# Merge, queries and everything behind as one stage, the queries' norm taken tile by tile

## The reference

```
n = rmsnorm(h); [ssd | gdn | gates] = n @ w_in
h += ( sigmoid(g_a) * (ssd_mixer(...) @ w_ssd_out)
     + sigmoid(g_b) * (gdn_mixer(...) @ w_gdn_out) ) @ w_out          # the merge
t = rmsnorm(h, norm_ffn)
qry = t @ w_query                                                     # 2048 wide
s = einsum(qry, sub_keys); top 16 of each half, top 16 of the 256 sums, softmax gate
h += sum over the chosen experts of  gelu(t . expert_u) * gate * expert_v
h += sigmoid(rmsnorm(h, norm_ple) @ w_ple_gate) * (p @ w_ple_proj);   y = rmsnorm(h)
```

## Time and profile before

| what | value |
|---|---|
| median of 3 runs | 2361.13 us (2359.95 to 2368.63) |
| the profiled execution | 2365.91 us |
| its span | 2364.0 us |
| TensorE busy | 2264.0 us (96%) |
| VectorE busy | 1542.0 us (65%) |
| GpSimd busy | 1205.3 us (51%) |
| ScalarE busy | 872.1 us (37%) |
| mean granted TensorE clock | 0.985 of full |

### The profile page before, as it was taken

One profiled execution on the slowest core, in us unless ns is written; L12 is line 12 of the kernel. 1 busy time (PEld: TensorE's weight loads), 2 busy tenths in 40 slices (PEclk: granted clock), 3 DMA queues, 4 the chain that ended last, 5 costly groups with the idle time before them and its releaser, 6 DMA issues.

```text
span 2364.0 us, 31147 instructions
## 1 busy us (share of the span) xinstructions
PE 2264.0 (96%) x10852; PEld 1883.7 (80%) x10852; DVE 1542.0 (65%) x3515; ACT 872.1 (37%) x1305; POOL 1205.3 (51%) x979
## 2 busy tenths in 40 slices
PE   8999899899989998899999999999999999999998
PEld 6787777788878886688888888888878888888885
DVE  4553688677764442119888888884238888887783
ACT  6454433244434331334333333333233323323342
POOL 3333465666544432324566666665647765555510
PEclk9999999999999999999999999999999999999999
DMA  4222011223345231324444444446449999999940
GB/s 166 89 82 79 19 45 40 82 86 128 133 150 180 89 125 36 127 78 126 143 146 147 147 147 141 145 144 215 147 143 384 392 382 347 364 347 356 355 188 36
DMA packets 160314, 394.61 MB, mean 167 GB/s; under 512 B 27376, under 2 KB 93168, under 8 KB 149872
## 3 DMA queue, kind: packets, MB, share of 16 engines
q1 hardware_dynamic: 125424, 326.32, 40.1%
q0 software_dynamic: 34816, 67.41, 7.6%
HBM read 328.45 MB, written 65.21 MB: 167 GB/s over the span
## 4 chain that ended last, share of the span: by engine, by line
PE 58%; DMA 0%; ACT 0%; issue 0%; DVE 0%; POOL 0%; DVEq 0%; SPq 0%
PE ps L182 10%; PE ps L181 10%; PE ps L180 10%; PE ps L2246 7%; PE ps L2247 7%; PE ps L2248 7%; PE ps L1316 4%; PE ps L1578 1%; PE ps L2298 1%; DMA query_slots_sb<-peer_query 0%; POOL query_low_sb L1284 0%; PE ps L2276 0%; DVE h_sb L2121 0%; ACT query_high_sb L1272 0%; DVE ple_gate_sb L2110 0%
## 5 line engine op out<-in xcount | busy, mean ns | idle before, releaser
L1801 POOL DMA_INDIRECT g_dense<-up_gates_summed_sb,up_gate_at_sb x384 | 418.9, 1091 | 300.7 <-issue 222.5
L180 PE MATMUL ps<-n_high_sb,up_u_high_sb 128*128 128x512 f32 x1024 | 398.4, 389 | 0.0
L182 PE MATMUL ps<-n_high_sb,up_u_low_sb 128*128 128x512 f32 x1024 | 398.4, 389 | 0.0
L181 PE MATMUL ps<-n_low_sb,up_u_high_sb 128*128 128x512 f32 x1024 | 398.3, 389 | 0.0
L2246 PE MATMUL ps<-down_v_high_sb,down_w_high_sb 128*128 128x512 f32 x768 | 300.2, 391 | 4.8 <-issue 4.8
L2247 PE MATMUL ps<-down_v_low_sb,down_w_high_sb 128*128 128x512 f32 x768 | 299.8, 390 | 0.0
L2248 PE MATMUL ps<-down_v_high_sb,down_w_low_sb 128*128 128x512 f32 x768 | 299.7, 390 | 0.0
L1660 DVE TENSOR_TENSOR up_u_low_sb<-up_u_sb,up_u_high_sb 128x1024 fp32r<-128x1024 f32 x128 | 156.6, 1224 | 159.0 <-ACT up_u_high_sb L1822 158.7
L2174 ACT ACTIVATE down_v_high_sb<-down_v_sb 128x1024 fp32r<-128x1024 f32 x120 | 125.8, 1048 | 310.4 <-PE ps L2248 310.4
L1834 ACT ACTIVATE up_gelu_sb<-ps 128x512 f32<-128x512 f32 x128 | 76.5, 598 | 406.5 <-PE ps L182 406.4
L181 PEld LDWEIGHTS ps<-n_low_sb,up_u_high_sb 128*128 128x128 f32 x1024 | 192.2, 188 | 39.9
(11 more groups left out here) (348 smaller groups left out, 4747.9 us busy)
## 6 DMA issues: line engine op xcount, KB each, us to landing
up_u_sb<-expert_u SPq DMA_DIRECT2D x128, 512.0 KB, 3.8
down_v_sb<-expert_v SPq DMA_DIRECT2D x32, 2048.0 KB, 11.9
a_dense<-up_gelu_sb SPq DMA_DIRECT2D x128, 256.0 KB, 2.2
g_dense<-nought_sb SPq DMA_DIRECT2D x8, 3072.0 KB, 10.7
down_gelu_sb<-a_dense SPq DMA_DIRECT2D x32, 768.0 KB, 4.8
down_gates_sb<-g_dense SPq DMA_DIRECT2D x32, 768.0 KB, 6.3
w_slots_sb<-w_conv SPq DMA_DIRECT2D x19, 1024.0 KB, 4.9
query_slots_sb<-peer_query SPq DMA_DIRECT2D x8, 1024.0 KB, 5.0
```

The lines of the kernel that those rows point to most:

```text
L180: pe.matmul(out, ah, bh, start=k == 0, stop=False)
L181: pe.matmul(out, ah, bl, start=False, stop=False)
L182: last = pe.matmul(out, al, bh, start=False, stop=k == n - 1)
L1801: pool.indirect_dma_start(cells, at, summed[:, tt, k:k + 1], None).then_inc(stored[tt], 16)
```

## The change

`merge_stage` becomes `merge_programs`: the same programs for the five engines, but handed to `down_stage`, where each engine runs its merge program ahead of its up program in the same block. The barrier between them goes. Waits take its place: query weights are loaded and their high parts made once the mixing products are done (`mixed_in`), the low parts once `m_low` is complete, and the keys once all merge products are done. The output product waits for merged tiles one by one. The norm of the queries is a new class, `FfnNorm`: the last four adds of the merge are made inside its program, each followed by that tile's square, mean, root, reciprocal and two half scalings. Its scaled tiles have memory of their own, so that the query weights don't overlap them. In the up part, the gelus of the first two down blocks are loaded at block 108, and the gates where both were loaded before.

```diff
-            def free_out(tt, p):
-                if tt == 0:
-                    pe.wait_ge(m_low, KT)
-            for p in (OUT, OUT + 1):
-                stream.pe(pe, p, 4 * (p - OUT), lambda tt: free_out(tt, p), (mh, ml), True)
+        merged = lambda kt: pe.wait_ge(m_low, kt + 1)
+        stream.pe(pe, OUT, 0, lambda tt: None, (mh, ml), True, merged)
+        stream.pe(pe, OUT + 1, 4, lambda tt: None, (mh, ml), True)
...
+class FfnNorm(NormT):
+    def act(self, act, merge):
+        m = self.m
+        for tt in range(TT):
+            act.wait_ge(merge.added, TT + tt + 1)
+            act.activation(self.xs[:, tt, :], m.h[:, tt, :], ACT.Square,
+                           accum_out=m.stat[:, 0, tt:tt + 1]).then_inc(self.sq_done, 1)
+            act.wait_ge(self.ms_done, tt + 1)
+            act.activation(m.stat[:, 2, tt:tt + 1], m.stat[:, 1, tt:tt + 1], ACT.Sqrt).then_inc(self.root_done, 1)
...
+    def dve(self, dve, merge):
...
+        def scale(tt):
+            dve.wait_ge(self.root_done, tt + 1)
+            st.done(dve.reciprocal(m.stat[:, 0, tt:tt + 1], m.stat[:, 2, tt:tt + 1]))
+            for half in range(2):
+                c = slice(half * CW, (half + 1) * CW)
+                dve.tensor_scalar(self.xs[:, tt, c], m.h[:, tt, c], m.stat[:, 0, tt:tt + 1], None, ALU.mult).then_inc(self.scaled, 1)
+
+        merge.add(dve, 1, 0)
+        mean(0)
+        scale(0)
+        merge.add(dve, 1, 1)
+        mean(1)
+        for tt in range(2, TT):
+            merge.add(dve, 1, tt)
+            scale(tt - 1)
+            mean(tt)
+        scale(TT - 1)
...
+    def pe(self, pe, merge):
...
+        for half in range(2):
+            for tt in range(TT - 1):
+                if half:
+                    pe.wait_ge(merge.added, 2 * TT)
+                else:
+                    pe.wait_ge(merge.added, TT)
+                pe.wait_ge(self.scaled, 2 * tt + 2)
+                for kt in range(half * KT // 2, (half + 1) * KT // 2):
+                    turn(tt, kt)
+        for kt in range(KT):
+            pe.wait_ge(self.scaled, 2 * (TT - 1) + 1 + kt // (KT // 2))
+            turn(TT - 1, kt).then_inc(self.turned, 1)
...
     def sp(self, sp):
-        sp.dma_start(self.keys[:, :, :], ...).then_inc(self.keys_in, 16)
-        self.stream.sp(sp)
+        def keys(n):
+            if n == 2:
+                sp.wait_ge(self.merge.prod, self.merge.all_products)
+                sp.dma_start(self.keys[:, :, :], ...).then_inc(self.keys_in, 16)
+
+        sp.wait_ge(self.merge.prod, self.merge.mixed_in)
+        self.stream.sp(sp, keys)
...
     def act(self, act, split):
-        self.norm.act(act, between=lambda: (self.stream.high(act, 0), self.stream.high(act, 1)))
+        act.wait_ge(self.merge.prod, self.merge.mixed_in)
+        self.stream.high(act, 0)
+        self.stream.high(act, 1)
+        self.norm.act(act, self.merge)
...
-            if j == WEIGHTS_AT:
+            if j == PREFETCH_AT + 2 * DOWN_J:
                 for n in range(RING):
                     sp.wait_ge(a_stored[n], 16 * (2 * DOWN_J // RING + 1))
+                for b in range(2):
+                    down.load_gelus(sp, b, b)
+            if j == WEIGHTS_AT:
                 for tt in range(DENSE):
                     sp.wait_ge(stored[tt], 16 * HK)
-                down.load_weights(sp, 0, 0)
+                down.load_gates(sp, 0, 0)
             if j == PEER_K - 2:
-                down.load_weights(sp, 1, 1)
+                down.load_gates(sp, 1, 1)
```

More of the change, by code:

```diff
@@ new lines, in add, with sync, gates, others @@
+    def add(dve, n, tt):
+        dve.wait_ge(prod, 4 * (OUT + n) + tt + 1)
+        v = m.h[:, tt, n * CW:(n + 1) * CW]
+        dve.tensor_tensor(v, v, m.ps[:, 4 * n + tt, :], ALU.add).then_inc(added, 1)
+    def sync(sp):
+        def gates(k):
+            if k >= 2:
+                sp.wait_ge(mixed, 4 * (k - 1))
+            for f in range(4):
+                sp.dma_start(sg[:, k % 2, f, :], m.gate_pre[4 * k + f]).then_inc(gate_in[k % 2], 16)
+        def others(n):
+            if n == 4:
+                gates(0)
+                gates(1)
+            if n == 6:
+                for tt in range(TT):
+                    x = m.ins["x_prompt"] if tt < TS else m.ins["x_sample"]
+                    sp.dma_start(m.h[:, tt, :], x[0, (tt % TS) * P:(tt % TS + 1) * P, :]).then_inc(h_in, 16)
+            if n in (2 * FIRST[1], 2 * FIRST[1] + 2):
+                gates(n // 2 - FIRST[1] + 2)
+        stream.sp(sp, others)
@@ new lines, in gpsimd, with tensor @@
+    def gpsimd(pool):
+        stream.pool(pool)
+    def tensor(pe):
+        for p in range(4):
+            stream.pe(pe, p, 4 * (p % 2), lambda tt: p < 2 or pe.wait_ge(silu, 4 * (p - 2) + tt + 1), n_x, True)
+        for a in range(2):
+            for kt in range(KT):
+                if a == 0:
+                    pe.wait_ge(silu, 9 + kt)
+                elif kt == 0:
+                    pe.wait_ge(mixed, 8)
+                if kt == 0:
+                    pe.wait_ge(scaled, TT * (a + 1))
+                for tt in range(TT):
+                    last = pe.transpose(m.ps[:, kt, tt * P:(tt + 1) * P], y[a][:, tt, kt * P:(kt + 1) * P], sq(m, "eye"))
+                last.then_inc(turned, 1)
+            for n in range(2):
+                free = lambda f: pe.wait_ge(t_out, KT * a + 4 * n + f + 1)
+                turned_in = lambda kt: n or pe.wait_ge(t_out, KT * a + kt + 1)
+                stream.pe(pe, FIRST[a] + n, 4 * n, free, (yh, yl), False, turned_in)
+        merged = lambda kt: pe.wait_ge(m_low, kt + 1)
+        stream.pe(pe, OUT, 0, lambda tt: None, (mh, ml), True, merged)
+        stream.pe(pe, OUT + 1, 4, lambda tt: None, (mh, ml), True)
@@ L1561, in pe @@
         m, norm = self.m, self.norm
-        norm.pe(pe)
+        norm.pe(pe, self.merge)
         normed = lambda k: pe.wait_ge(norm.out_done, k + 1)
@@ L1604, in dve @@
     def dve(self, dve):
-        self.norm.dve(dve)
+        self.norm.dve(dve, self.merge)
         for g in range(4):
@@ L1649, in up_stage @@
     exp_at = []
-    query = Query(nc, m)
+    query = Query(nc, m, merge)
     def vector(dve):
@@ L1972, in _ @@
         def _(sp):
+            merge.sync(sp)
             up.sync(sp)
```

289 lines of the change are left out of this document (136 added, 153 removed).

## The result

| | before | after |
|---|---|---|
| median of 6 runs | 2361.63 us (2359.15 to 2368.63) | 2347.64 us (2337.85 to 2348.70) |
| the profiled execution | 2365.91 us, span 2364.0 | 2347.61 us, span 2345.8 |
| mean granted clock | 0.985 | 0.991 |

The kernel is faster: the ratio after to before is 0.9927, 95% interval 0.9914 to 0.9940, which is 17.2 us of 2361 (14.2 to 20.3). I had said 24.1. The six times of after stand in two groups, 2337.85 and 2338.84, which is 0.9 and 1.8 above the forecast of 2337.0, and four from 2347.61 to 2348.70. The profiled execution is of the upper one.

A forecast was written before the change was run, and what follows sets the result against it. TensorE, busy for 96% of the span, was taken as the bound, so only its gaps could be won. 11.7 + 9.5 - 1.3 + 2.9 + 1.3 = 24.1 us off the median of 2361.1 gives 2337.0; range 2331 to 2346.

The forecast's parts named there:

- forecast: Whole kernel: all parts of the change work, 24.1 us less, median 2337.0 us; chance 0.72.
- Step 1: Output product of the merge: waiting tile by tile removes the gap and half clock behind it, 11.7 us (9.3 to 11.7).
- Step 2: Seam from last output to first query product: early query weights, then the norm decides; 16.66 becomes 7.2, gain 9.5 (8.8 to 10.2).
- The 1.3 us that I took off: Query products: half of a 2.6 us half-clock loss behind the short groups of transposes, bounds 0 and 2.6.
- Rival B: Merge-query seam: query weights still arrive last, step 2 gives some 2 us, total 17.9, time 2343; chance 0.06.
- The table load: ScalarE in the queries' norm: 1.28 us as in the trace, without the skill page's added drain of about 1.38.
- Step 3: Start of the down part: gelus loaded early, gates first; gap 4.8 to 1.9, gain 2.9, plus 1.3 of clock.
- Case A: Down part's start: nothing net, gates no sooner or third block's low parts make TensorE wait; total 19.9, time 2341; chance 0.16.
- The clock rival D: Query products: short transpose groups keep TensorE at 1.2 GHz, making the kernel slower; all 384 matmuls 77 us, 2414; chance 0.02.

The follow-up runs named there:

- e1: The changed kernel measured again, unaltered: median 2349.14 us, ratio to the kernel before 0.9918.
- e4: The kernel before with only the waits by merged tile added: median 2355.21 us, ratio 0.9951.
- e8: The changed kernel with the query weights asked for only behind the last output product: median 2371.29 us, ratio to the kernel before 1.0030.
- e2: The changed kernel without early loads, its first down gelus and gates loaded together and late: median 2342.02 us, ratio to the kernel before 0.9903.
- e6: The changed kernel with VectorE waiting for its own last write behind each low weight part: median 2341.28 us, ratio to the kernel before 0.9897.
- e3: The kernel before with only the early loads of the gelus added: median 2366.84 us, ratio 1.0006.
- e11: The changed kernel without early loads, VectorE waiting for its own last write behind each low weight part: median 2340.62 us, ratio to the kernel before 0.9906.
- e9: The changed kernel with the third down block split ahead of the first block's rows, later ones as they were: median 2337.60 us, ratio to before 0.9908.
- e12: The kernel before with VectorE waiting for its own last write behind each low weight part: median 2362.00 us, ratio 1.0005.

## Why the prediction was right, and where it failed

The direction was right, and the case (forecast) is the one that runs of the lower group show, at 2338. The median, 2347.64, is above the forecast and 1.6 above the range's upper end. That the lower group comes so near to 2337.0 is in part luck. From the span of before to that of e1 it is 26.8 us, not 24.1; the profile of before lies 4.8 us above its median, and in e1 the gap at the first down product is gone altogether, since the scatters happened to end early. Step by step:

**Step 1 was right.** The last output product came 11.5 us earlier (946.73 to 935.24) in a profile whose merge started 0.2 later; 11.7 was booked, and e4 measures it alone at 11.6 (8.3 to 14.9). No half clock followed.

**Step 2 was right in mechanism, and a little small.** 16.66 became 6.13 where 7.2 was booked, so the gain is 10.5, just past the bound of 10.2. Add 3 started at 935.85 (booked 935.9), and the first half of tile 3 was scaled at 938.86 (booked 938.9). The rest is the clock: it never fell. The last 24 transposes took 2.81 us, 0.94 for eight (booked 0.88 at full clock and 1.5 at half), and the query products ran at full. The 1.3 us that I took off were not lost. The early weights passed the three queues in time, and e8 shows that they had to: 22 us hang on it. Rival B, which let the norm run beside the late weights, had that path wrong and gave it 6.2.

**The table load** took 929.40 to 930.69, 1.29 us from load to root, as in the earlier trace rows. The 1.38 us of drain that the Trainium skill adds ("ScalarE: Activation LUTs", "What ACT_TABLE_LOAD costs") are not in this trace either.

**Step 3, the gates' own path, was nearly right in the profile.** They were issued at 1734.82, VectorE started 5.5 us later (4.9 booked), the gap fell to 2.56 (1.9 booked), and the clock stayed full, so 2.2 + 2.6 us came back where 4.2 were booked. But it is not a steady gain. It needs the gates to be late, and that hangs on when the scatters end, which moves by 15 us between executions: only 4 of 14 profiles have that gap at all, before, after, e2 and e6. Over many runs e3 (1.0006), e2 against e1, and e11 against e6 find nothing.

**The step that failed** is the end of step 3: "They hang on GpSimd's gathers, which waited for the last gelu [...] I take nothing off and count a wait here into the lower bound." The sum has no term for that wait: the lower end, 9.3 + 8.8 - 2.6 + 0.4 + 0 = 15.9, books nothing for it, whatever the sentence says. Case A had the same place and held 0.16, but it allowed only for the loss of the 4.2 us won there. The profile shows 6.71 us of wait there and 1.6 of half clock behind it, 8.3 in all, most of the 9 to 10 us between the groups. I counted only that everything comes 3 us forward together, against a slack of 0.7. That much came true: the first gather starts 26.15 us earlier than before and the up part ends 22.07 earlier, which leaves 4.1. What I did not see is that with the gates and gelus in hand VectorE does the work of the first two blocks in one stretch of 12.1 us (1740.36 to 1752.49), where before it had a hole of 1.9 us between the first block's split and the second's gates:

```profile
1770.39 1.97 DVE L2033 TENSOR_TENSOR down_gelu_sb<-down_gelu_sb,down_gates_sb 128x384 f32<-128x384 f32 x4 [1.90 <-DMA down_gates_sb<-g_dense]
```

GpSimd's first gather falls into that stretch and, in the profile of after, ends only behind it.

That this is the cause is shown by e6 for the profiled case: a gap in VectorE's stretch ends the gather. That every run at 2348 has such a gather is not shown: one execution of that group was profiled. The 13 runs with gaps, none of them there, speak for it; one run of e2 at 2349.51, two of e9 at 2345.7 and 2346.0, and the upper times that e12 keeps speak for a further cause, which is open. The Trainium skill names such a contention in "GPSIMD Engine Reference", "Key points": GpSimd shares its SBUF interfaces with VectorE and contends with instructions that have two SBUF inputs. The runs agree as to kind: the stretch is all `TENSOR_TENSOR` with two SBUF inputs, and held gathers end 0.74 to 0.86 us behind its first gap. They also show what the rule does not tell, since e1's first gather began in such a stretch and took 1.31 us, as most do. What lets one through and holds the next is open.

The clock rival D had the right caution and the wrong size: no stretch of query products ran at 0.50.

## What to carry to other kernels

Where a change brings work forward, look at the slack of the block after next, and at what else the engine in front of it is then doing: here VectorE's back to back stretch held one GpSimd gather for 8 us in one of two profiles, and a wait of VectorE for its own last write let such a gather through. Measure the parts alone as well: without the early loads (e2) the change does no worse. A gap that hangs on where a long row of indirect transfers happens to end is no gain to book; look at it in more than one execution. And when a barrier goes, ask first which queue the next weights stand in: with late weights (e8) the seam takes 28.5 us, more than the 16.7 that it took with the barrier.

## What the hardware showed that I had not expected

- A gather on GpSimd that takes 0.93 to 0.97 us alone, and mostly 0.9 to 2.0 under VectorE's two-input instructions, took 2.2 to 8.03 us in 22 cases of 3584, and these ended 0.74 to 0.86 us behind VectorE's first gap or the end of its stretch. A gap of 0.04 us sufficed.
- It goes the other way too: in e8 a scaling of 128x512 on VectorE took 4.19 us instead of 0.49 while GpSimd subtracted 128x2048 tiles, and ended 0.29 us behind GpSimd's.
- The 384 scatters end at quite different times from one execution to the next: the last at 1733.55 in after and at 1718.18 in e1, the same program, 15.4 us apart.
- TensorE's granted clock stayed at full (2.4 GHz) over the seam's gaps of 1.16 and 0.89 us, with small transposes between them, and over the gap of 2.56 us; it fell, to half at first, behind those of 4.8, 6.71 and 9 us, behind the 4.4 of e2 (0.67 over the next 5.1 us) and the 3.31 of e11 (0.63 over the next 4.2). The length of the gap does not settle it: in e4 a wait of only 1.90 us at the third block was followed by half clock (0.50 from 1788.6 to 1792.0), and the one of 2.46 in e12 was not (1.00 from 1798.7 to 1804).
